# A sixth weight slot, two late slots, and an earlier start of the second mixer's projections in a two-layer hybrid decoder

## What is computed

```python
for i in range(DEPTH):                       # 2
    h = rmsnorm(x, norm_mix_g[i])
    x = x + (mlstm_mixer if i % 2 == 0 else gla_mixer)(h, ...)
    h = rmsnorm(x, norm_ffn_g[i])
    x = x + jnp.square(jax.nn.relu(h @ w1[i])) @ w2[i]
return rmsnorm(x, final_norm_g)

def gla_mixer(xn, w_in, w_gate_up, b_gate, out_norm_g, w_out):
    q, k, v, r, z_low = jnp.split(xn @ w_in, ...)        # 512 | 512 | 1024 | 1024 | 16
    log_a = jax.nn.log_sigmoid(z_low @ w_gate_up + b_gate) / 16
    o = head_rmsnorm(gla_chunkwise(q * 128**-0.5, k, v, log_a), out_norm_g)
    return (jax.nn.silu(r) * o) @ w_out
```

## Time and profile before

| | us |
|---|---|
| median of 6 runs | 1432.39 |
| lowest to highest | 1430.69 to 1437.74 |
| the profiled execution's own time | 1432.77 |
| its span (slowest core, core 4) | 1431.7 |
| spans of the eight cores | 1408.7 to 1431.7 |
| TensorE busy on core 4 | 1330.4 (93%) |
| DVE, ACT, POOL busy on core 4 | 953.7, 748.0, 244.6 |

### The profile page before, as it was taken

The page is one execution under the profiler, slowest core; times in us unless marked ns, Lnnn a source line. Parts: engine busy times, 40 slices in busy tenths (PEclk is TensorE's granted clock), DMA queues, the critical chain, the costliest instruction groups (busy, mean ns, idle before and its releaser), DMA issues.

```text
span 1431.7 us, 23024 instructions; the slowest of 8 cores (1408.7 to 1431.7 us)
## 1 busy us (share of the span) xinstructions
PE 1330.4 (93%) x6703; PEld 625.0 (44%) x6821; DVE 953.7 (67%) x2079; ACT 748.0 (52%) x1589; POOL 244.6 (17%) x262
## 2 busy tenths in 40 slices
PE   6999999899999999999968999999899999989997
PEld 2455454444444444443433445444344444434445
DVE  3498485956479865586557777678554787885735
ACT  2486565535176273382356566664441853833545
POOL 5021021211111021111112002040111111111115
PEclk9999999999999999999998999999999999999999
DMA  9943112275685586659453101032757865876673
GB/s 165 246 112 76 31 38 37 41 83 74 82 100 72 73 103 79 80 68 159 70 114 93 34 20 30 16 56 30 89 67 87 98 74 70 106 136 112 83 99 119
DMA packets 203002, 118.85 MB, mean 83 GB/s; under 512 B 53968, under 2 KB 188288, under 8 KB 202880
## 3 DMA queue, kind: packets, MB, share of 16 engines
q0 software_dynamic: 143216, 91.40, 47.3%
q1 hardware_dynamic: 58576, 25.46, 7.8%
q10 hardware_dynamic: 1088, 0.52, 0.1%
HBM read 176.46 MB, written 8.39 MB: 129 GB/s over the span
## 4 chain that ended last, share of the span: by engine, by line
PE 76%; DMA 11%; DVE 5%; issue 4%; ACT 2%; POOL 1%; SPq 0%; DVEq 0%; ACTq 0%; POOLq 0%
PE ps L254 76%; DMA wraw_68<-w 3%; DMA wv<-m_win 2%; DMA wraw_69<-w 2%; DMA ktok_82<-kT 1%; DMA wraw_70<-w 1%; DMA wraw_71<-w 1%; DMA wraw_72<-w 1%; DMA wraw_73<-w 1%; DVE NB L972 1%; ACT ps L260 0%; DVE Cbf L1096 0%; DVE R_90 L268 0%; DVE xT L264 0%; POOL sd L264 0%
## 5 line engine op out<-in xcount | busy, mean ns | idle before, releaser
L264 DVE TENSOR_TENSOR xT<-ps,xT 128x512 f32<-128x512 f32 (+2 forms) x224 | 143.3, 649 | 127.2 <-PE ps L254 125.5
L260 ACT ACTIVATE ps<-ps 128x512 f32<-128x512 f32 x176 | 102.5, 585 | 201.1 <-PE ps L254 194.1
L260 ACT ACTIVATE rt<-ps 128x512 f32<-128x512 f32 x125 | 73.9, 592 | 83.1 <-PE ps L254 82.6
L260 ACT ACTIVATE sq<-xT 128x512 f32<-128x512 f32 x136 | 83.4, 625 | 43.1 <-DVE sd L264 21.7
L264 POOL TENSOR_TENSOR sd<-sd,sq 128x512 f32<-128x512 f32 x50 | 63.8, 1276 | 43.7 <-ACT sq L260 35.8
L260 ACT ACTIVATE junk<-ps 128x256 bf16<-128x256 f32 x128 | 49.0, 383 | 27.3 <-DVE ps L264 12.7
L268 DVE SCALAR_TENSOR_TENSOR R_90<-R_90,egs,ps 128x256 f32<-128x256 f32 x112 | 53.0, 473 | 14.3 <-PE ps L254 13.0
L264 POOL TENSOR_TENSOR sd<-sq 128x512 f32<-128x512 f32 x10 | 13.0, 1297 | 288.2 <-ACT sq L260 279.2
L211 POOL DMA_DIRECT2D wraw_68<-w x27 | 23.8, 881 | 174.6 <-PE ps L254 75.2
L211 POOL DMA_DIRECT2D wraw_69<-w x26 | 22.9, 881 | 149.1 <-PE ps L254 78.7
L211 POOL DMA_DIRECT2D wraw_70<-w x23 | 20.2, 880 | 162.1 <-PE ps L254 80.0
(11 more groups left out here) (580 smaller groups left out, 3575.4 us busy)
## 6 DMA issues: line engine op xcount, KB each, us to landing
wraw_68<-w POOLq DMA_DIRECT2D x27, 512.0 KB, 8.3
wraw_69<-w POOLq DMA_DIRECT2D x26, 512.0 KB, 7.6
wraw_72<-w POOLq DMA_DIRECT2D x26, 512.0 KB, 7.9
wraw_71<-w POOLq DMA_DIRECT2D x24, 512.0 KB, 7.3
wraw_70<-w POOLq DMA_DIRECT2D x23, 512.0 KB, 7.7
outT<-xT SPq DMA_DIRECT2D x12, 512.0 KB, 4.1
xT<-xT POOLq DMA_DIRECT2D x6, 512.0 KB, 32.2
xT<-xT SPq DMA_DIRECT2D x5, 512.0 KB, 4.6
```

The lines of the kernel that those rows point to most:

```text
L260: t.op("act", lambda e: e.activation(out=out, in_=in_, func=func, **kw), r=r, w=w, ns=190 + 0.84 * n + (80 if acc is not None else 0))
L264: t.op(eng, lambda e: e.tensor_tensor(out=out, in0=in0, in1=in1, op=op), r=r, w=w, ns=170 + 1.03 * n if eng == "dve" else 200 + 2.2 * n)
```

## The change

- A sixth slot for the whole of both MLPs. `XS[4]` now takes the place of `XS[2]` (it is written over it once the plain tiles are done), so `XS` is seven blocks long and leaves 4 KB free behind it for slot 5. Its sums lie where four `tmp` buffers were; two `tmp` are kept, so the MLP has six.
- Two further slots (6 and 7) over `XS[5]` to `XS[7]`, for layer 0's last down steps, when `XS` is no longer read. The slots of the last eight slabs are (4, 5, 0, 1, 6, 7, 5, 0).
- Since `XS[2]` is gone, the last four up steps of layer 1 are in Winograd's form too.
- Layer 1's group 1 is normalised in the last down steps of layer 0's MLP, like group 0. Its sums of squares are made by TensorE (`stats_pe`) instead of DVE and POOL. Group 0's sums start ten steps sooner.
- `wv` is loaded in three DMAs (3, 3 and 2 blocks) after the last slab. Ahead of v and o stand, behind q and k of group 0: the scores of chunk 0, the decay factors of group 1 for two heads, and q and k of group 1 for two heads. The other two heads are filled into chunks 0 and 1.

```diff
-    XP = (0, 1, 2, 3, 6, 7, 4, 5)
+    XP = (0, 1, 2, 3, 2, 4, 5, 6)
...
-    slots = [XO + i * SLAB for i in range(5)] + [W[1] + 8192]
...
+    slots = [(XO + i * SLAB, [XO + i * SLAB + 4096 + j * 1024 for j in range(3)]) for i in range(5)]
+    slots += [(W[1] + 12288, [M + 24576 + j * 1024 for j in range(3)]),
+              (W[1], [W[1] + 4096 + j * 1024 for j in range(3)]), (W[1] + 7168, [W[1] + 11264, M + 27648, KT1])]
...
-    tmp = [rt[:, i, :] for i in range(4)] + [at("tmp%d" % i, [128, GS], F32, M + 24576 + i * 2048)[0][:] for i in range(4)]
+    tmp = [rt[:, i, :] for i in range(4)] + [at("tmp%d" % i, [128, GS], F32, M + 28672 + i * 2048)[0][:] for i in range(2)]
...
+    def stats_pe(g):
+        def f(k0):
+            if k0 == 0:
+                ring["held"][g] = nb()
+                ring["banks"] = [x for x in ring["banks"] if x != ring["held"][g]]
+            stats_direct(g, range(k0, k0 + 4), ring["held"][g])
+            if k0:
+                rstd_fin(ring["held"][g])
+        return [lambda: f(0), lambda: f(4)]
...
-                sl["prev"] = last.get(sl["slot"], -1 if sl["slot"] < 5 else n - 2)
+                sl["prev"] = last.get(sl["slot"], -1)
...
                 if c == 0:
-                    return x[:2] + o + x[2:] + v + (qk(2)[1:] if s.m else [])
+                    return x[:2] + o + x[2:] + v + (qk(2)[1:] if s.m else s.z(1, 1) + qk(2) if s.pre else [])
                 if c == 1:
                     if s.m:
                         return o + qk(3)[1:]
-                    return x[:2] + o + qk(0) + qk(1) + s.z(1, 1) + x[2:] + v
+                    return x[:2] + o + (qk(3) if s.pre else qk(0) + qk(1) + s.z(1, 1)) + x[2:] + v
                 if c == 2:
-                    return o + v + ([] if s.m else qk(2) + qk(3))
+                    return o + v + ([] if s.m or s.pre else qk(2) + qk(3))
...
-                    steps.append(dict(kind="up", pair=pair, P=P0 + p, p=p, wino=UPW[layer][pair] and not fin, done=0,
+                    steps.append(dict(kind="up", pair=pair, P=P0 + p, p=p, wino=UPW[layer][pair], done=0,
...
-    SLOTS = ((0, 1, 2, 3, 4), (3, 4, 0, 1, 2))
-    ffn = [Ffn(0, lambda n: (1, 5, 4, 0)[n % 4] if n >= 56 else SLOTS[0][n % 5], ffn_steps(0)),
-           Ffn(1, lambda n: SLOTS[1][n % 5], ffn_steps(1))]
+    SLOTS = ((0, 1, 2, 3, 4, 5), (3, 4, 0, 1, 2, 5))
+    ffn = [Ffn(0, lambda n: (4, 5, 0, 1, 6, 7, 5, 0)[n - 56] if n >= 56 else SLOTS[0][n % 6], ffn_steps(0)),
+           Ffn(1, lambda n: SLOTS[1][n % 6], ffn_steps(1))]
...
-        ring["tmps"] = range(8)
+        ring["tmps"] = range(6)
...
-    hooks[43] = [fewer_tmp]
-    hooks[44] = stats_slots(0, "dve") + [lambda: load_cols(wqk, "wqk", g_win_d, 0, 4)]
-    hooks[45] = xn_slots(1, 0, m1.gcol) + [lambda: load_cols(wv, "wv", g_win_d, 1024, 4, range(4))]
-    hooks[46] = [lambda: m1.zl_F(0), lambda: m1.z_F(0, 0)]
+    m1.pre = True
+    hooks[34] = [lambda: sq_half(0, 0, "dve")]
+    hooks[35] = [lambda: sq_half(0, 1, "dve")]
+    hooks[43] = [fewer_tmp, lambda: sq_sum(0)]
+    st1 = stats_pe(1)
+    hooks[44] = xn_slots(1, 0, m1.gcol) + [lambda: load_cols(wqk, "wqk", g_win_d, 0, 4, range(4)), st1[0]]
+    hooks[45] = [st1[1], lambda: load_cols(wqk, "wqk", g_win_d, 0, 4, range(4, KC)), lambda: m1.zl_F(0),
+                 lambda: m1.z_F(0, 0)]
+    hooks[46] = xn_slots(1, 1, m1.gcol)
+    hooks[47] = [lambda: load_cols(wv, "wv", g_win_d, 1024, 3, range(6))]
     F0.run(2, len(F0.steps), hooks)
-    load_cols(wv, "wv", g_win_d, 1024, 4, range(4, KC))
+    load_cols(wv, "wv", g_win_d, 1024, 2, range(6, KC))
     load_cols(wo, "wo", g_win_d, 2048, 4)
...
+    m1.zl_F(1)
     set_ring(RING["g"])
-    for fn in m1.v(0):
-        fn()
     m1.S1(0)
     m1.KX(0)
     m1.KX(1)
-    for fn in m1.o(0) + m1.v(1):
+    m1.z_F(1, 0)
+    for fn in m1.qk(1, 0) + m1.qk(1, 1) + m1.v(0) + m1.o(0) + m1.v(1):
         fn()
```

More of the change, by code:

```diff
@@ L305, in build @@
     cur[0] += 32768
-    slots = [XO + i * SLAB for i in range(5)] + [W[1] + 8192]
-    wraw = [at("wraw%d" % i, [128, 8, 2, 128], BF16, o)[0] for i, o in enumerate(slots)]
-    wsum = [at("wsum%d" % i, [128, 3, 4, 128], BF16, o + 4096)[0] for i, o in enumerate(slots)]
+    KT1 = cur[0]
+    cur[0] += 1024 + PAD
+    slots = [(XO + i * SLAB, [XO + i * SLAB + 4096 + j * 1024 for j in range(3)]) for i in range(5)]
+    slots += [(W[1] + 12288, [M + 24576 + j * 1024 for j in range(3)]),
+              (W[1], [W[1] + 4096 + j * 1024 for j in range(3)]), (W[1] + 7168, [W[1] + 11264, M + 27648, KT1])]
+    wraw = [at("wraw%d" % i, [128, 8, 2, 128], BF16, o[0])[0] for i, o in enumerate(slots)]
+    wsum = [[at("wsum%d_%d" % (i, j), [128, 4, 128], BF16, a)[0] for j, a in enumerate(o[1])]
+            for i, o in enumerate(slots)]
     qTm, _ = at("qT", [128, H, GS], BF16, M)
     kTm, _ = at("kT", [128, 4, H, CH], BF16, M + 4096)
-    KT = [M + 8192, cur[0]]
-    cur[0] += 1024 + PAD
+    KT = [M + 8192, KT1]
     ktok = [at("ktok%d" % i, [128, H, DK], BF16, KT[i])[0] for i in range(2)]
@@ L390, in build @@
             t.reg(("xs", i, j), W[0] + XP[i] * 4096 + j * 1024, 1024)
-    for i, o in enumerate(slots):
+    for i, (o, o1) in enumerate(slots):
         t.reg(("wr", i), o, 256, 8, 512)
@@ L395, in build @@
         for j in range(3):
-            t.reg(("ws", i, j), o + 4096 + j * 1024, 1024)
+            t.reg(("ws", i, j), o1[j], 1024)
     for i, nm in enumerate(("wqk", "wv", "wo", "wout")):
@@ L426, in build @@
         t.reg(("rt", i), RT + i * 2048, 2048)
-        t.reg(("rt", 4 + i), M + 24576 + i * 2048, 2048)
+        if i < 2:
+            t.reg(("rt", 4 + i), M + 28672 + i * 2048, 2048)
     t.reg(("zl",), SQ, 2048)
@@ L450, in nb @@
             a = nb()
-            mm(PB[a][:], ones_bf[:], XS[0][:, 0, :], [("xs", 0, 0), ("ones_bf",)], [("B", a)], True, True, True, 512)
+            mm(PB[a][:], ones_bf[:], sqb[:], [("sqb",), ("ones_bf",)], [("B", a)], True, True, True, 512)
             ring["full"].add(a)
@@ L604, in sums @@
                 A = lambda a, c: wraw[i][:].rearrange("p (i c) a n -> p i c a n", c=2)[:, :, c, a, :]
-                S = lambda j: wsum[i][:, j, :, :]
+                S = lambda j: wsum[i][j][:]
                 R, W3, WS = ("wr", i), ("w3", i), lambda j: ("ws", i, j)
@@ L615, in left @@
             return {1: (lambda k: raw[:, 2 * k, 0, :], ("wr", i)), 2: (lambda k: raw[:, 2 * k + 1, 0, :], ("wr", i)),
-                    3: (lambda k: sm_[:, 2, k, :], ("ws", i, 2)), 4: (lambda k: raw[:, 2 * k + 1, 1, :], ("wr", i)),
-                    5: (lambda k: sm_[:, 0, k, :], ("ws", i, 0)), 6: (lambda k: sm_[:, 1, k, :], ("ws", i, 1)),
+                    3: (lambda k: sm_[2][:, k, :], ("ws", i, 2)), 4: (lambda k: raw[:, 2 * k + 1, 1, :], ("wr", i)),
+                    5: (lambda k: sm_[0][:, k, :], ("ws", i, 0)), 6: (lambda k: sm_[1][:, k, :], ("ws", i, 1)),
                     7: (lambda k: raw[:, 2 * k, 1, :], ("w3", i))}[q]
@@ L829, in __init__ @@
             s.gcol = layer * 8
+            s.pre = False
         def qk_buf(s, g):
@@ L1172, in run @@
                     if g == 0:
-                        if c == 0:
+                        if c == 0 and not s.pre:
                             for fn in [] if s.m else st + xs:
@@ L1369, in fewer_tmp @@
     def fewer_tmp():
-        ring["tmps"] = range(4, 8)
+        ring["tmps"] = range(4, 6)
     F0 = ffn[0]
```

## The result

The changed kernel takes **1387.7 us** (median of 10 runs; 1431.9 before, 20 runs). The ratio is 0.9691, 95% interval 0.9676 to 0.9706: 44 us less. Forecast were 1404, with 1394 to 1420.

What follows compares the result with a forecast made beforehand. TensorE bounds the kernel, with time gained where it idles, runs at half clock or has less work; for core 2, 1427.5 - 17.7 - 7 - 1.75 + 1.5 = 1402.6, then 1403.7, say 1404 us; range 1394 to 1420.

Steps and rivals of the forecast that it cites:

- Part 1, the mixer: Start of the GLA mixer: matmuls moved ahead fill TensorE's idle and half-clock time; gain 17.7 us, bounds 11.7 to 20.
- the cover for `wo`: Mixer start: second wo load lands about 18.6 us after first issue, TensorE reaches it after about 21; 2 us to spare.
- the 5 us that I left for idle time: Mixer start: of 22.7 us lost, 5 us were taken to stay; best case 2.7, worst 11.
- Part 2, the slots: Both MLPs: six slots end waits hanging on slabs in mid-MLP; 0 to 13.9 us on core 4, 12 taken.
- the sum: Part 2's slab waits on core 4: 6.2 us in layer 0's MLP plus 7.7 in layer 1's, 13.9 us.
- The mechanism that I did name: MLPs: a slab issued late makes DVE wait (3.00 us), its sum is late, and TensorE loses 1.52 us.
- The 8.3 us of the earlier trace: Median time of a slab load on the page before, used against the skill's 4.4 us estimate to value the sixth slot.
- Part 3: Layer 1's last up steps: 16 matmuls fewer, 8 more for sums of squares; -1.75 us.
- Part 4: Scarcer buffers: six tmp for eight cost nothing; two PSUM banks held in layer 0's last down steps; 1.5 us taken.
- the forecast's own range: Range of the forecast case: 1396 (all of part 2, residue 2.7) to 1411 us (residue 11).
- I lowered the gain for core 2: Core 2's part 2 in the MLPs was put at most at 9 us, 7 taken, making it slowest at 1402.6.
- The forecast wait at the start of layer 1's MLP: Wait of 4.43 us for layer 1's fourth slab, not counted as gain; about 4 us was to remain.

Runs made afterwards that it cites:

- e1_five: The changed kernel with five slots in the cycle of both MLPs for six; ratio 0.9825, profiled 1406.0 us.
- e3_planlate: The changed kernel, six slots, with the planner taking every slab to land 11 us later; ratio 0.9873, profiled 1416.2 us.
- e11_plan3: The changed kernel, six slots, with the planner taking slabs to land 3 us later; ratio 0.9664.
- e6_tmp5: The changed kernel with five tmp buffers in the MLPs for six; ratio 0.9705.
- e5_vfirst: The changed kernel with v and gate of chunk 0 and v of chunk 1 ahead of group 1's q and k; ratio 0.9709, profiled 1389.4 us.
- e7_early: The changed kernel with the sixth slot third in layer 0's cycle, fourth in layer 1's, and layer 1's fourth slab loaded sooner; ratio 0.9663.

## Why the prediction was right in direction and wrong in size

*Part 1, the mixer: right.* -17.7 forecast, -19.6 measured. No wait on ktok, full clock behind the MLP, and the cover for `wo` 2.3 us for 2. Of the 5 us that I left for idle time, 1.4 are there between 700 and 790 us.

*Part 2, the slots: this step failed.* I took the waits that name a slab, or that DVE's wait for a slab led to, as all that the sixth slot could end: "Each wait that hangs on a slab in the middle of an MLP should go", 13.9 us at most. The waits on `xT` and on ACT's copies at the ends of steps, 19 of 0.2 to 1.7 us on core 4 with 15.1 us together, stand in no term of the sum: I put them at nothing, and gave no reason. On core 2 after the change four of them are left, with 1.7 us. They hung on the slot as well, by way of the planner's order: e1_five brings them back in their old sizes, e3_planlate brings back waits of that kind with nearly all slabs landed. So the slot is worth 18 to 22 us, for the 12 of the sum on core 4 and the 7 on core 2.

The mechanism that I did name was only half true. DVE's waits were to vanish; they stayed (60.8 us for 57.6 in both MLPs), and e11_plan3, which removed most of them, was no faster. TensorE's direct waits on slabs fell from 10.7 to 4.4 us; the sum had 5.3 of these 6.3. The 8.3 us of the earlier trace rows are the median of one slot; the other four on that page have 7.3 to 7.9.

*Part 3: as worked out.* In layer 1's MLP busy time fell by 7.4 us: 3.5 are the 16 matmuls, 2.65 the half clock of the earlier trace rows that is gone, 1.2 stay open. *Part 4: small, as taken*; with five buffers e6_tmp5 is 2 us off, within the noise. The two PSUM banks have no run of their own. The lower end of the forecast's own range leaves out the 1.1 us between span and time: 1431.7 - 20 - 13.9 - 1.75 + 1.1 is 1397, not 1396.

*The slowest core.* I lowered the gain for core 2. But the slow cores gained 43 to 54 us, the others 28 to 35. In the MLPs core 1 had been idle for 10.4 and 14.0 us where core 4 was for 20.8 and 24.3; now both are at 11.3 or less. The waits on `xT` and ACT's copies had been the same on both (15.6 and 15.1 us). What core 4 had more of were those on loads (10.7 us for 0.7) and on `rt` and `tmp` (12.9 for 5.7); of both together 8.6 and 5.0 us are left. So the maximum over the cores fell by more than a typical core did. The 16 us are thus not the slot's alone. Averaged over the cores it gave 18.3 us where the sum had 12 or 7, the mixer 20.4 where it had 17.7, and layer 1's MLP 4.6 beside the slot, of which 3.5 are the 16 matmuls; start and end took 2.8, and the rest is the narrower spread of the cores.

*Not seen:* the end of the program is 2.1 us longer. In the chain that ended last, 3.15 us of ACT's queue (a store's issue, which took 0.42 us before) now stand ahead of the last norm's inverse square root. In e5_vfirst and e7_early, with another order, the end is as short as before.

The forecast wait at the start of layer 1's MLP is there: 4.37 us at 989.73 on core 2.

## What to carry to other kernels

Where a planner orders an in-order engine, a buffer that comes free sooner changes the order, and the wait that it ends may name neither the buffer nor its load. So read a short wait at a step's end by asking what could have stood in the gap, and why it did not; the order of both kernels, side by side at that place, can show this before any run. And here a planner's landing time was better a little late than a little early: 3 us late cost nothing, 2 us early 33 us (and 11 us late 26 to 32).

## What was not expected of the hardware

Loads that are issued together land one after the other. Four slabs asked for between 302.39 and 304.99 on core 2 landed 6.5, 11.0, 13.2 and 22.0 us after their issue, one alone (344.46) after 5.6. So a slab's time depends on how many were released with it. Before, three slabs were asked for at this place, and the last of them landed 12.6 to 16.0 us after its issue, by core; with the sixth slot's load second in the row, the last of four took 16.4 to 22.0. The estimate of 4.4 us from the Trainium skill, "DMA: Bandwidth & Descriptors", section "Anatomy of one DMA — SWDGE (gpsimd) path", is 1.2 us under the load that went alone; for those of a burst the measurement decides. The last of the four is what DVE stands 5.19 us for at 327.10, and TensorE 4.38 us at 332.80: here the sixth slot costs something.
